# Linear-attention chunk loop: sigmoid and query decays kept in PSUM, key decay by one biased exponential, outputs ahead of the third pair of level products

## What is computed

```python
bc_all = jnp.cumsum(to_chunks(gk), axis=-2)
def step(S, inp):
    qc, kc, vc, bc = inp
    diff = bc[..., :, None, :] - bc[..., None, :, :]
    decay = jnp.exp(jnp.where(causal[:, :, None], diff, -jnp.inf))
    A = jnp.einsum('bhid,bhijd,bhjd->bhij', qc, decay, kc)
    o = jnp.einsum('bhij,bhjv->bhiv', A, vc) + jnp.einsum('bhid,bhdv->bhiv', qc * jnp.exp(bc), S)
    blast = bc[..., -1:, :]
    S = S * jnp.exp(blast[..., 0, :])[..., None] + jnp.einsum('bhjd,bhjv->bhdv', kc * jnp.exp(blast - bc), vc)
    return S, o
...
o = rms_norm(o, gla_g) * jax.nn.silu(g_out.reshape(B, T, GLA_HEADS, GLA_DV).astype(F32))
```

## Time and profile before

| | |
|---|---|
| three timed runs | 3351.40, 3351.47 (median), 3362.22 us |
| profiled execution | 3344.12 us, of it a span of 3342.3 us |
| TensorE clock granted, mean | 0.98 |
| busy, share of span | TensorE 95%, VectorE 48%, ScalarE 33%, GpSimd 5% |
| GLA loop in the span | from 243 to 369 us |

### The profile page before, as it was taken

How to read it: one execution, slowest core, us unless ns; L and a number is a source line. 1 busy time by engine, 2 the same in 40 slices (tenths; PEclk the granted TensorE clock), 3 DMA queues, 4 the chain that set the end, 5 groups by cost and what they waited for, 6 DMA issues and landing times.

```text
span 3342.3 us, 45005 instructions
## 1 busy us (share of the span) xinstructions
PE 3178.9 (95%) x17766; PEld 2595.1 (78%) x17766; DVE 1618.1 (48%) x2434; ACT 1087.3 (33%) x2050; POOL 161.9 (5%) x272
## 2 busy tenths in 40 slices
PE   7998899999999999999999799989999999999997
PEld 5687697777888888877788688869777788888886
DVE  6277637336333333357655466644632733333336
ACT  3343445235221222234221256634423522212122
POOL 0018200000000000000000011100000000000000
PEclk9999899999999999999999899989999999999998
DMA  3110231001111111111222221113100111111112
GB/s 121 35 45 20 80 123 51 26 26 45 44 47 47 44 50 50 50 51 63 101 95 94 82 61 53 51 45 115 44 25 26 51 51 51 44 44 47 47 44 76
DMA packets 80740, 189.17 MB, mean 57 GB/s; under 512 B 6240, under 2 KB 39280, under 8 KB 80112
## 3 DMA queue, kind: packets, MB, share of 16 engines
q1 hardware_dynamic: 40320, 141.91, 13.5%
q10 hardware_dynamic: 40304, 45.64, 4.0%
HBM read 166.55 MB, written 20.97 MB: 56 GB/s over the span
## 4 chain that ended last, share of the span: by engine, by line
PE 84%; DVE 10%; ACT 3%; issue 2%; DMA 1%; DVEq 0%; ACTq 0%; SPq 0%
PE ps L2037 55%; PE ps L2053 14%; PE ps L2400 2%; PE ps L2184 2%; PE ps L2164 1%; DVE work L1211 1%; PE ps L2341 1%; DVE hres L1242 1%; DVE work L1227 1%; PE ps L2524 1%; DMA wraw<-wstream_dram 1%; PE ps L2405 1%; PE ps L2304 1%; PE ps L2507 1%; ACT whi L570 1%
## 5 line engine op out<-in xcount | busy, mean ns | idle before, releaser
L2037 PE MATMUL ps<-act,whi 128*128 128x512 f32 x3712 | 1182.5, 400 | 33.0 <-DVE wlo L1195 16.6
L2037 PEld LDWEIGHTS ps<-act,whi 128*128 128x128 f32 x3712 | 704.6, 191 | 201.5 <-DVE wlo L1195 19.5
L2037 PE MATMUL ps<-act,wlo 128*128 128x512 f32 x1856 | 734.6, 396 | 0.0
L2037 PE MATMUL ps<-hid,whi 128*128 128x512 f32 x2048 | 637.3, 393 | 3.5 <-DVE work L1483 2.2
L570 ACT ACTIVATE whi<-wraw 128x1024 fp32r<-128x1024 f32 x262 | 276.6, 1058 | 932.8 <-DMA wraw<-wstream_dram 932.0
L1195 DVE TENSOR_TENSOR wlo<-wraw,whi 128x1024 fp32r<-128x1024 f32 x257 | 314.5, 1225 | 465.2 <-ACT whi L570 462.3
L2037 PEld LDWEIGHTS ps<-hid,whi 128*128 128x128 f32 x2048 | 384.2, 188 | 89.0 <-DVE wlo L1195 4.7
L2037 PEld LDWEIGHTS ps<-act,wlo 128*128 128x128 f32 x1856 | 353.6, 191 | 78.4
L2037 PE MATMUL ps<-hid,wlo 128*128 128x512 f32 x1024 | 398.1, 389 | 0.0
L2053 PE MATMUL ps<-act,whi 128*128 128x512 f32 x1408 | 379.5, 391 | 7.4 <-DVE work L1585 4.3
L2053 PEld LDWEIGHTS ps<-act,whi 128*128 128x128 f32 x1408 | 264.9, 188 | 65.9 <-issue 9.5
(11 more groups left out here) (271 smaller groups left out, 3255.1 us busy)
## 6 DMA issues: line engine op xcount, KB each, us to landing
wraw<-wstream_dram SPq DMA_DIRECT2D x262, 512.0 KB, 3.5
qkvz<-work ACTq DMA_DIRECT2D x32, 512.0 KB, 2.6
work<-qkvz ACTq DMA_DIRECT2D x64, 256.0 KB, 3.3
hres<-xT_dram ACTq DMA_DIRECT2D x8, 512.0 KB, 12.1
hres<-xT_dram ACTq DMA_DIRECT2D x1, 4096.0 KB, 12.1
outT_dram<-hres SPq DMA_DIRECT2D x16, 256.0 KB, 2.0
work<-memT_dram ACTq DMA_DIRECT2D x2, 1024.0 KB, 4.9
work<-masks_in_dram ACTq DMA_DIRECT2D x1, 1024.0 KB, 15.1
```

The costliest lines, as they stand in the source:

```text
L2037: last = mm(out_of(u)[:, 0:width], (wlo if hl else whi)[s][:, at:at + P], rhs(kt, xp, e), start=kt == hl == xp == 0, stop=kt == kts - 1 an ...
```

## The change

- The sigmoid's last step writes PSUM bank 7 instead of `work` 18, and the gated product reads it there. TensorE therefore waits, before the next gate's products enter bank 7, for the gated product (`sig_done`) instead of the scaling (`evac`).
- The query decay exp(b) is written to the upper half of bank 5 (`eq`), by a step of its own on ScalarE (`query_decays`) after the copies of the transposes and the state update of the chunk before; the decayed queries become VectorE's last step of a chunk and the outputs wait for them.
- The key decay is exp(last - b) in one step on ScalarE, from b, with the last column as bias and scale -1, one instruction per head pair; the subtractions L495 and L1659 go.
- TensorE: the 6 + 6 gate products around output and pair 2 become 12 behind pair 2. VectorE: the gated product moves ahead of the state update.
- SP: the load into the slot that shares memory with b waits for the last query decay instead of the last transposes.

```diff
-        gsel = Steps(sem("gla_select"), "q L0 L1 L2 L3")
+        gqd = Steps(sem("gla_query_decay"), "q")
+        gsel = Steps(sem("gla_select"), "L0 L1 L2 L3 q")
...
-            "E": [in_lin(j * 9 * W2, 9, 2, CH) for j in range(2)],
+            "E": [in_lin(j * 8 * W2, 8, 2, CH) for j in range(2)],
...
+            "eq": bank(5)[:, W2:2 * W2].rearrange("p (h n) -> p h n", h=2),
...
-                        sp.wait_ge(gpe.sem, gpe.at("tr", NCH - 1))
+                        sp.wait_ge(gqd.sem, gqd.at("q", NCH - 1))
...
-                gprep.done(tt(e[:, 7], b[:, :, CH - 1:CH].to_broadcast([P, 2, CH]), b, ALU.subtract), "b")
+                gprep.done(last, "b")
...
                 def decays_b(c):
-                    e, at = gla["E"][c % 2], slice(c * CH, (c + 1) * CH)
-                    eng.wait_ge(gsel.sem, gsel.at("q", c - 2))
-                    A(e[:, 8], work[:, 16:18, at], ACT.Exp)
-                    A(gla["decay"][c % 4], work[:, 16:18, (c + 1) * CH - 1:(c + 1) * CH], ACT.Exp)
+                    e, b = gla["E"][c % 2], work[:, 16:18, c * CH:(c + 1) * CH]
+                    for hp in range(2):
+                        A(e[:, 7, hp], b[:, hp], ACT.Exp, scale=-1.0, bias=b[:, hp, CH - 1:CH])
+                    A(gla["decay"][c % 4], b[:, :, CH - 1:CH], ACT.Exp)
                     eng.wait_ge(gprep.sem, gprep.at("b", c))
-                    gexp.done(A(e[:, 4:8], e[:, 4:8], ACT.Exp), "b")
+                    gexp.done(A(e[:, 4:7], e[:, 4:7], ACT.Exp), "b")
+
+                def query_decays(c):
+                    eng.wait_ge(gstate.sem, gstate.at("S", c - 1))
+                    gqd.done(A(gla["eq"], work[:, 16:18, c * CH:(c + 1) * CH], ACT.Exp), "q")
...
                     eng.wait_ge(evac, ug + c + 1)
-                    eng.wait_ge(sig_done, c)
                     link(A(gla["sig"], uh(4 + t, e), ACT.Exp, scale=-1.0))
                     link(A(gla["sig"], gla["sig"], ACT.Ln, bias=one_col))
-                    A(gla["sig"], gla["sig"], ACT.Exp, scale=-1.0).then_inc(sig_ready, 1)
+                    A(bank(7), gla["sig"], ACT.Exp, scale=-1.0).then_inc(sig_ready, 1)
...
                         token_major(c)
+                        query_decays(c)
...
                 def decayed_queries(c):
-                    eng.wait_ge(gexp.sem, gexp.at("b", c))
+                    eng.wait_ge(gqd.sem, gqd.at("q", c))
                     eng.wait_ge(gfin.sem, gfin.at("o", c - 2))
-                    gsel.done(TT(gla["QE"][c % 2], gla["E"][c % 2][:, 8], work[:, 12:14, c * CH:(c + 1) * CH], ALU.mult),
-                              "q")
+                    gsel.done(TT(gla["QE"][c % 2], gla["eq"], work[:, 12:14, c * CH:(c + 1) * CH], ALU.mult), "q")
...
-                    TT(uh(4 + t, e), uh(4 + t, e), gla["sig"], ALU.mult).then_inc(sig_done, 1)
+                    TT(uh(4 + t, e), bank(7), uh(4 + t, e), ALU.mult).then_inc(sig_done, 1)
...
                         gate(c)
-                        decayed_queries(c)
                         select(c, 0)
                         select(c, 1)
+                        gated(c)
                     if c:
                         state(c - 1)
                     if c < NCH:
                         select(c, 2)
-                        gated(c)
                         select(c, 3)
+                        decayed_queries(c)
...
-                    eng.wait_ge(gsel.sem, gsel.at("L3", c))
+                    eng.wait_ge(gsel.sem, gsel.at("q", c))
...
-                            eng.wait_ge(evac, plan.need[u] + 1)
+                            eng.wait_ge(sig_done, c)
...
                         pair(c, 0)
                         pair(c, 1)
-                        if more:
-                            gate(c + 1, (0, 1))
                     if c:
                         output(c - 1)
                     if c < NCH:
                         pair(c, 2)
                         if more:
-                            gate(c + 1, (2, 3))
+                            gate(c + 1, (0, 1, 2, 3))
```

More of the change, by code:

```diff
@@ L1149, in mixer1 @@
                 split_hi(plan.at["out1"][0] + 3)
-            for s in (gexp, gev, gout, *pact, *fact, *oact):
+            for s in (gexp, gqd, gev, gout, *pact, *fact, *oact):
                 s.credit(eng)
@@ L1658, in first_decays @@
                             gprep.done(last, "a")
-                    gprep.done(TT(e[:, 7], b[:, :, CH - 1:CH].to_broadcast([P, 2, CH]), b, ALU.subtract), "b")
+                    gprep.done(last, "b")
                 for c in range(2):
```

## The result

| | before | changed |
|---|---|---|
| timed runs, median | 3351.59 us (5) | 3330.22 us (5) |
| lowest to highest | 3351.40 to 3362.22 | 3328.13 to 3331.83 |
| profiled execution | 3344.12, span 3342.3 | 3328.13, span 3326.3 |

The ratio is 0.9927, with a 95% interval from 0.9912 to 0.9942: 0.7% faster. I had forecast 3328 and a range of 3315 to 3344. One later run of the kernel before took 9046.35 us; it counts as a slow one and enters no ratio.

A forecast was written before the change was run, and what follows sets the result against it. TensorE, busy 95% of the span, was stalled by a VectorE product held off by GpSimd's SBUF reads. Gains 19.5 + 1.2 less losses 1.2 and 0.2 gave 19.3 us, from 3344.12 to 3324.8; forecast median 3328, range 3315 to 3344.

The forecast's parts named there:

- (a): Sigmoid to PSUM: VectorE's gated product takes 0.69 us instead of being held by GpSimd, a gain of 19.5 us.
- (b): Query decays to PSUM: VectorE's decayed queries fall to 0.415 us, worth nothing since VectorE has slack in the chunk.
- (c): Key decay by biased exponential: GpSimd loses 3.7 us, ScalarE adds two exponentials of 0.3; all beside TensorE, GpSimd narrowly ahead.
- (d): TensorE's gate products in 12 + 12 instead of 6 + 6 + 12: 0.2 us less per chunk, a gain of 1.2 us.
- (e): TensorE's gate products wait for the gated product: 0.65 us to spare in steady chunks; chunk 0 loses 1.2, bounds 0.9 to 3.
- (f): Last chunk: outputs start 10.2 us into it instead of 10.0, a loss of 0.2 us.
- (g): On SP, the fourth output block's load waits for the last query decay: costs nothing, at worst 2.2 us.
- The 7 us between the profiled execution and the median before: Timed median 7.35 us above the profiled run: 3325 if from longer holds, 3332 if from elsewhere; 3328 taken between.
- the first: Rival: GpSimd becomes the pace, one microsecond lost in each of 6 chunks, 3331 to 3338 us; chance 0.12.
- The second: Rival: VectorE's hold is not tied to the second SBUF input, the 19.5 us stay, 3344 to 3351 us; chance 0.10.
- The third: Rival: TensorE's new wait lands in every chunk and drops the clock, 6.5 us each, 3370 us; chance 0.06.

The follow-up runs named there:

- experiment 2: Changed kernel with the sigmoid written to SBUF and read from there, everything else as changed: 3375.72 us, ratio 1.0056.
- experiment 8: Changed kernel with only the query decays back in SBUF: 3343.88 us, ratio 0.9980.
- experiment 1: Kernel before with the sigmoid in PSUM, the gated product early and gate products in 12 + 12; query and key decays as before: 3353.19 us, ratio 0.9986.
- experiment 9: Changed kernel with the key decay's subtraction and common exponential put back as before: 3330.51 us, ratio 0.9934.
- experiment 6: Changed kernel with three more 128x256 subtractions on GpSimd in each of six decay preparations, 1.7 us per chunk: 3338.12 us, ratio 0.9945.
- experiment 4: Kernel before with the sigmoid in PSUM and the gated product early, but TensorE's old order of gate products: 3357.32 us, ratio 1.0002.
- experiment 7: Changed kernel run again without edits, in another group of runs: 3328.79 us, ratio 0.9940.
- experiment 3: Kernel before with GpSimd waiting for its own completion at four points per chunk, nothing moved to PSUM: 3331.70 us, ratio 0.9920.
- experiment 10: Changed kernel with the sigmoid in SBUF and GpSimd waiting for its own completion at four points per chunk: 3328.50 us, ratio 0.9936.
- experiment 11: Changed kernel with the sigmoid in SBUF and GpSimd waiting for its own completion once per chunk, after its operands: 3364.31 us, ratio 1.0048.

## Why the prediction was right

The time and the mechanism held: VectorE's product with two SBUF inputs was what held the loop, and moving its input to PSUM ended that. Experiments 2 and 8 undo one input each and bring the holds back. Experiment 1 has only one of the two inputs moved, and nothing is gained.

One reading in the prediction was wrong. It took GpSimd's stop at 277.99 as what ended the long hold at 277.67. The product ended 0.32 us ahead of that stop. Counted back from its end, its own 0.69 us begin at 276.98, just when L514 began, and L514 then took 1.01 instead of 0.46. The 7.59 us of chunk 6 ended in the same way: the product's last 0.69 us began at 337.20, with this instruction of GpSimd, which took 0.94 instead of 0.40 and was followed by others without a stop:

```profile
337.20 0.94 POOL L492 TENSOR_TENSOR lin<-work 128x128 f32<-128x128 f32 x1
```

So both holds of the kernel before ended while GpSimd ran on. Why there, no run shows. By the prediction's steps:

- **(a), 19.5 us: right, 19.6 measured** over chunks 1 to 6, but these belong to (a), (b) and (d) together.
- **(b), "worth nothing": wrong.** The step took the 415 to 682 ns of L1674 as the whole of what it could cost. They were only how often it had met GpSimd badly in one execution. Without (b) the kernel is at 3353 us with GpSimd as before (experiment 1) and at 3344 with the rest of the change (8), so (b) is worth 15 us or more once (a) is there. My bound should have been that of (a): the same two inputs, the same neighbour. That (b) was part of the change was luck for the forecast: the same working would have given 3328 for experiment 8's kernel, which took 3343.88.
- **(c), beside TensorE: right** (experiment 9). GpSimd is only narrowly ahead, as worked out: of 10.3 us more in six chunks, 5 to 7 show in the loop (experiment 6). Of ScalarE's prices, the two 128x128 exponentials were 0.39 each against my 0.3, and L918 with its result in PSUM took 0.60 us where L913 took 0.63. The Trainium skill, page "ScalarE: Activation LUTs", section "Step-by-step: what each stage is for", calls PSUM the lower-latency destination; the two rows agree, by 0.03 us.
- **(d), 1.2 us: wrong, nothing measured.** A chunk takes 13.30 us, as before. The 12 gate products in a run do take 2.96 us, but the first product pair of the outputs, which now follows level products, takes 0.42 us where it took 0.22 behind gate products. From these rows the 0.2 us is paid at each change from level products (64 rows) to full ones (128): a run of 6 took 1.59 us and one of 12 took 2.95, so 0.23 each and 0.2 once. There are three such changes in either order.
- **(e), the steady chunk: right.** The gated product runs 4.2 to 4.9 us into a chunk (262.89 to 263.58, of a chunk that starts at 258.65), and from chunk 1 to 6 TensorE never waits for it. Experiment 4 prices the uncovered wait at 3.1 us against my 2.9. **Chunk 0: mis-sized, 3.3 us instead of 1.2**, just outside my bound of 3. The gate products began 5.1 us into the chunk, not 4.5: the selections started only after the first pair's products (at 1.1, not 0.9), four of them took 3.1 us, not 2.9, and 0.14 us passed behind the gated product. The twelve gate products then ran at a mean granted clock of 0.55 and took 4.52 us instead of 2.97. That the clock could fall here I had only in the bound; in experiment 7, where it didn't, the loss is 1.8 us.
- **(f), a loss of 0.2: wrong in sign, a gain of 1.0.** The outputs start 10.7 us into the chunk, later even than my 10.2. But they ran at full clock now, 0.22 us a pair; before, most pairs took 0.42 or 0.43 us, in a stretch with a mean granted clock of 0.61.
- **(g), nothing: right**, as the time from the last state update to the end is the same to 0.1 us.

My sum gave 3324.8 for the profiled execution, and it was 3328.1: 2.1 us from chunk 0, 1.2 from (d) and 1.3 from a dip of the clock ahead of the loop, less 1.2 from (f) and 0.1 from (a). That these misses partly cancel is luck. The 7 us between the profiled execution and the median before I had split; the changed kernel's median is 2.1 us above its profiled run, so some 5 of the 7 us would have gone with the holds. That is argued, but it fits the spread: the runs of the kernel before lie mostly between 3342 and 3366 us, all nine of the changed kernel between 3327 and 3336.

Of the rivals, the first (GpSimd sets the pace) is real and near, as experiments 3, 6 and 10 show, but did not come. The second (the hold isn't tied to the SBUF input) is refuted by experiment 8, which moves one operand and nothing else. The third, a new wait in each chunk with the clock behind it, did not come. Experiment 4 has such a wait, but from TensorE's old order and not from a late GpSimd, and it costs 25 to 29 us and not 45.

## What to carry to other kernels

Ask of each two-input VectorE instruction beside a busy GpSimd whether one of its inputs can be in PSUM, and move all of them or none: with one left, the holds moved there, and all or two thirds of the gain were gone (experiments 1 and 8). The time that such an instruction took in one profile is no bound for it; its inputs and its neighbour are. Where GpSimd runs long rows, try a few waits for its own completion first: four of them did as much here as the whole change, though why they work is open, and they cost GpSimd its lead over TensorE. And what a buffer moved to PSUM makes others wait for has to be covered by an order, in the first round of a loop too.

## What the runs showed of the hardware

- A VectorE instruction with two SBUF inputs can be held off through some 30 GpSimd instructions. Of 18 holds of over 5 us, 16 ended at a stop of GpSimd, be it only the pause of 0.08 us of experiment 11: 0.28 us after its last instruction for 256 columns (experiments 1 and 8), 0.55 for 512 (experiment 2: 252.62 after 252.07). The other two, 14.56 and 7.59 us in the kernel before, ended while GpSimd ran on. The Trainium skill (page "SBUF — State Buffer", section "SBUF: two separate sides") has the loser blocked for the whole instruction of the other. That fits the passing products (0.7 to 1.0 us beside instructions of 0.46, 1.2 to 2.8 beside weight remainders of 2.38) and not the held ones.
- What decides between passing and being held stays open. It isn't the instant within GpSimd's instruction: started 0.30 us after one, a product was held in experiment 2 (247.25 after 246.95) and passed in experiment 10 (290.89 after 290.59). Waits of GpSimd for its own completion, four per chunk, made all 15 gated products pass that met GpSimd at work (experiments 3 and 10); one per chunk did not, but let in a product that was held when it came (experiment 11). That four work is shown; how is not.
- When a product got in while GpSimd ran on, GpSimd paid: beside a product of 512 columns its next instruction took 0.79 to 1.01 us and not 0.40 or 0.46.
- In chunk 0, behind two stops of TensorE of some 0.8 and 1.1 us, the granted clock fell to half in the changed kernel's execution (twelve gate products of 4.52 us in all, at a mean of 0.55) and in that of experiment 9 (4.48 us), and not in those of experiments 7 and 8 (3.01 and 2.98 us).
